# Expert weights of a mixture-of-experts stage in 8 KB runs: two rows for each of two experts per transfer, in place of one row for each of four

## The reference

```python
def _ec_moe(h, w_router, w_gate, w_up, w_down):
    B, L, _ = h.shape
    cap = EC_FACTOR * L // N_EXPERTS
    aff = jax.nn.softmax((h @ w_router).astype(jnp.float32), axis=-1)
    vals, idx = lax.top_k(jnp.swapaxes(aff, 1, 2), cap)
    bidx = jnp.arange(B)[:, None, None]
    xs = h[bidx, idx]
    hid = jax.nn.silu(jnp.einsum('becd,edf->becf', xs, w_gate)) * jnp.einsum('becd,edf->becf', xs, w_up)
    y = jnp.einsum('becf,efd->becd', hid, w_down) * vals[..., None].astype(h.dtype)
    return jnp.zeros_like(h).at[bidx, idx].add(y.astype(h.dtype))
```

## Time and profile before

| what | value |
|---|---|
| median of 3 runs | 1529.62 us (1526.79 to 1532.09) |
| profiled execution, its own time | 1532.12 us |
| profiled execution, its span | 1530.1 us |
| mean granted TensorE clock | 0.933 of full |
| TensorE matmul busy | 1292.4 us, 84% of the span |
| VectorE, ScalarE, GpSimd busy | 637.5, 498.0, 106.8 us |
| moved by DMA | 376.69 MB, of which 201 MB are expert weights |

### The profile page before, as it was taken

How to read it: one execution, slowest core, us unless ns; L and a number is a source line. 1 busy time by engine, 2 the same in 40 slices (tenths; PEclk the granted TensorE clock), 3 DMA queues, 4 the chain that set the end, 5 groups by cost and what they waited for, 6 DMA issues and landing times.

```text
span 1530.1 us, 22584 instructions
## 1 busy us (share of the span) xinstructions
PE 1292.4 (84%) x9336; PEld 960.6 (63%) x9336; DVE 637.5 (42%) x941; ACT 498.0 (33%) x756; POOL 106.8 (7%) x117
## 2 busy tenths in 40 slices
PE   5999999875555555655699999999999999999997
PEld 2388667521111111111477999999999987999996
DVE  2625665400100100100377656556545448566554
ACT  2424424400000000000437544445343438544443
POOL 0010010100000000000037000000000018000000
PEclk8999999898888887877899999999999999999999
DMA  9533619999999999999832465665566741355662
GB/s 366 201 97 83 237 71 356 418 409 418 419 419 419 418 419 421 416 420 420 306 111 70 152 193 165 186 199 164 179 191 183 216 141 57 109 168 168 198 198 68
DMA packets 137966, 376.69 MB, mean 246 GB/s; under 512 B 9423, under 2 KB 56960, under 8 KB 137703
## 3 DMA queue, kind: packets, MB, share of 16 engines
q1 hardware_dynamic: 137894, 375.68, 67.9%
HBM read 373.55 MB, written 1.05 MB: 245 GB/s over the span
## 4 chain that ended last, share of the span: by engine, by line
PE 64%; DMA 25%; DVE 4%; ACT 3%; SPq 2%; POOL 1%; issue 1%; ACTq 0%; DVEq 0%
PE psum L1937 16%; PE psum L1939 16%; PE psum L1938 16%; DMA ring<-in_w_down 6%; DMA work<-in_w_gate 4%; DMA work<-in_w_up 3%; PE psum L2278 3%; DMA ring<-in_w_up 3%; DMA tokens<-in_w_down 3%; DMA ring<-in_w_gate 3%; SPq L579 1%; PE psum L1873 1%; DMA early<-in_w_up 1%; POOL work L763 1%; PE psum L2107 1%; PE psum L2375 1%
## 5 line engine op out<-in xcount | busy, mean ns | idle before, releaser
L1937 PE MATMUL psum<-parts 128*128 128x256 f32 (+1 forms) x1672 | 497.2, 297 | 11.7 <-DVE parts L1585 9.5
L1938 PE MATMUL psum<-parts 128*128 128x256 f32 (+1 forms) x1672 | 494.8, 296 | 0.0
L1939 PE MATMUL psum<-parts 128*128 128x256 f32 (+1 forms) x1672 | 494.7, 296 | 0.0
L1579 DVE TENSOR_TENSOR parts<-ring,parts 128x1024 fp32r<-128x1024 f32 x232 | 280.8, 1227 | 170.7 <-ACT parts L1047 170.0
L1937 PEld LDWEIGHTS psum<-parts 128*128 128x128 f32 x1672 | 322.2, 193 | 22.5 <-issue 13.9
L1938 PEld LDWEIGHTS psum<-parts 128*128 128x128 f32 x1672 | 322.4, 193 | 7.1
L1939 PEld LDWEIGHTS psum<-parts 128*128 128x128 f32 x1672 | 322.1, 193 | 7.3
L1047 ACT CAST parts<-ring 128x1024 fp32r<-128x1024 f32 x232 | 239.6, 1045 | 249.1 <-PE psum L1939 209.3
L2278 PE MATMUL psum<-ring,work 128*32 128x512 f32 x576 | 95.8, 801 | 75.8 <-DMA ring<-in_w_gate 31.1
L1037 ACT ACTIVATE work<-psum 128x1024 f32<-128x1024 f32 x4 | 4.1, 1023 | 382.0 <-PE psum L2278 382.0
L1562 DVE TENSOR_TENSOR work<-work,psum 128x1024 f32<-128x1024 f32 x4 | 4.9, 1221 | 266.1 <-ACT work L1037 266.1
(11 more groups left out here) (357 smaller groups left out, 1396.8 us busy)
## 6 DMA issues: line engine op xcount, KB each, us to landing
ring<-in_w_qkv_b SPq DMA_DIRECT2D x72, 512.0 KB, 4.3
ring<-in_w_gate SPq DMA_DIRECT2D x16, 2048.0 KB, 22.2
work<-in_w_up SPq DMA_DIRECT2D x12, 2048.0 KB, 23.3
ring<-in_w_down SPq DMA_DIRECT2D x12, 2048.0 KB, 23.3
ring<-in_w_ada SPq DMA_DIRECT2D x44, 512.0 KB, 8.1
ring<-in_w_gate SPq DMA_DIRECT2D x44, 512.0 KB, 3.9
ring<-in_w_up SPq DMA_DIRECT2D x44, 512.0 KB, 5.3
ring<-in_w_down SPq DMA_DIRECT2D x44, 512.0 KB, 4.3
```

What stands on the lines that cost most here:

```text
L1579: dve.tensor_tensor(part_of(lo_slots, t, n), ring[:, slot_2(t), 0:n], part_of(hi_slots, t, n), ALU.subtract).then_inc(lo_ready, 1)
L1937: pe.matmul(out, lhsT[0], rhs[0], start=start, stop=False, skip_group_check=True)
L1938: pe.matmul(out, lhsT[0], rhs[1], start=False, stop=False, skip_group_check=True)
L1939: return pe.matmul(out, lhsT[1], rhs[0], start=False, stop=stop, skip_group_check=True)
```

## The change

The eight rows `8p` to `8p+7` of a weight matrix now belong to partition `p`, so that rows `8p + 2i` and `8p + 2i + 1`, which lie behind each other in HBM, are one run of 8 KB. A quad is still 2 MB, but holds two such rows for each of two experts: quads come in pairs (experts 0 and 1, experts 2 and 3), and a pair holds what contraction steps `2i` and `2i+1` need for all four experts. `by_expert` therefore takes two quads at once, runs the matmuls of two steps and adds eight to `tiles_done` at their end.

The rest follows the row order: contraction step `k` is now the rows `8c + k`. Transposes of `xn` and `hd`, the two `mod` calls for the feed-forward scale and shift, and the view `xn_by_k` read every eighth column (32 bytes apart) where they read neighbouring ones. The router's weights load as one run per partition. The host-side columns for gain and bias are laid out accordingly.

```diff
-        xn_by_k = [xn[:, t].rearrange("p (k c) -> p k c", k=KD) for t in range(TT)]
+        xn_by_k = [xn[:, t].rearrange("p (c k) -> p k c", k=KD) for t in range(TT)]
...
-                    sp.dma_start(w_rout, d["w_router"][0].rearrange("(k p) e -> p k e", p=P)).then_inc(route_loaded, 16)
+                    sp.dma_start(w_rout, d["w_router"][0].rearrange("(p k) e -> p k e", p=P)).then_inc(route_loaded, 16)
...
             def load_quad(expert, q):
-                name, k = (("w_gate", "w_up")[q % 2], q // 2) if q < 2 * KD else ("w_down", q - 2 * KD)
+                both, half = q // 2, q % 2
+                name, pair = (("w_gate", "w_up")[both % 2], both // 2) if both < KD else ("w_down", both - KD)
                 out, full, _ = homes[home_of[q]]
-                sp.dma_start(out, d[name][0, bass.ds(expert, EG), P * k:P * k + P, :].rearrange("j p n -> p j n")).then_inc(full, 16)
+                rows = d[name][0, bass.ds(expert + 2 * half, 2), :, :].rearrange("j (p r) n -> p j (r n)", r=KD)
+                sp.dma_start(out.rearrange("p j n -> p (j n)").rearrange("p (j m) -> p j m", j=2),
+                             rows[:, :, 2 * D * pair:2 * D * pair + 2 * D]).then_inc(full, 16)
...
-            def turn(src, ready, bank=0):
+            def turn(src, ready, bank=0, by_eights=False):
...
-                        ins = pe.transpose(ps[bank + k // 2][:, at:at + P], src[:, t, P * k:P * k + P], ident[:, :])
+                        rows = src[:, t].rearrange("p (c k) -> p k c", k=KD)[:, k, :] if by_eights else src[:, t, P * k:P * k + P]
+                        ins = pe.transpose(ps[bank + k // 2][:, at:at + P], rows, ident[:, :])
...
-                    ins = pe.matmul(ps[MOD_BANK[i]][:, 2 * k:2 * k + 2], modrow[:, P * k:P * k + P], pick_row, start=True, stop=True)
+                    row = modrow[:, P * k:P * k + P] if i < 2 else modrow.rearrange("p (c k) -> p k c", k=KD)[:, k, :]
+                    ins = pe.matmul(ps[MOD_BANK[i]][:, 2 * k:2 * k + 2], row, pick_row, start=True, stop=True)
...
-                def by_expert(bank, lhsT, w, k):
-                    for n in range(2):
-                        for j in range(EG):
-                            rows = slice(CAP * j, CAP * j + CAP)
-                            ins = pe.matmul(ps[bank + n][rows, :], lhsT[:, k, rows], w[:, j, 512 * n:512 * n + 512],
-                                            start=(k == 0), stop=(k == KD - 1))
-                    ins.then_inc(tiles_done, EG)
+                def by_expert(bank, lhsT, pair):
+                    ws = [quad(), quad()]
+                    for k in (2 * pair, 2 * pair + 1):
+                        for n in range(2):
+                            for j in range(EG):
+                                rows = slice(CAP * j, CAP * j + CAP)
+                                w = ws[j // 2][:, 2 * (j % 2) + k % 2, 512 * n:512 * n + 512]
+                                ins = pe.matmul(ps[bank + n][rows, :], lhsT[:, k, rows], w, start=(k == 0), stop=(k == KD - 1))
+                    ins.then_inc(tiles_done, 2 * EG)
...
-                for k in range(KD):
-                    by_expert(0, xs, quad(), k)
-                    by_expert(2, xs, quad(), k)
+                for pair in range(KD // 2):
+                    by_expert(0, xs, pair)
+                    by_expert(2, xs, pair)
...
-                    ins = pe.transpose(ps[6 + k // 4][:, P * (k % 4):P * (k % 4) + P], hd[:, P * k:P * k + P], ident[:, :])
+                    ins = pe.transpose(ps[6 + k // 4][:, P * (k % 4):P * (k % 4) + P], hd.rearrange("p (c k) -> p k c", k=KD)[:, k, :], ident[:, :])
...
-                for k in range(KD):
-                    by_expert(4, hdT, quad(), k)
+                for pair in range(KD // 2):
+                    by_expert(4, hdT, pair)
```

More of the change, by code:

```diff
@@ L2213, in _ @@
             pe.wait_ge(x_mixed, TT)
-            turn(xn, xt_ready, X_BANK)
+            turn(xn, xt_ready, X_BANK, by_eights=True)
             pe.wait_ge(route_loaded, 48)
@@ L2586, in laid_out @@
     column(C_GMIX, a["norm_mix_g"][0])
-    column(C_GFFN, a["norm_ffn_g"][0])
+    cols[:, C_GFFN:C_GFFN + KD] = a["norm_ffn_g"][0].reshape(P, KD)
     column(C_MIX2, a["norm_mix_2"].reshape(-1))
@@ L2593, in laid_out @@
     column(C_ADA, a["b_ada"][0])
+    for m in (3, 4):
+        cols[:, C_ADA + KD * m:C_ADA + KD * m + KD] = a["b_ada"][0][D * m:D * m + D].reshape(P, KD)
     column(C_FIN1, a["norm_final_g"])
```

## The result

The changed kernel takes 1537.67 us (median of 6 runs, 1537.37 to 1539.93) where the kernel before takes 1529.76 (6 runs): ratio 1.0061, with an interval of 1.0048 to 1.0074. It is slower, and outside the forecast range.

The account below looks back on a forecast made before the run. The prediction took the expert stage to run at the pace of the DMA engines, with slack in TensorE. Its terms, -10.3 + 3.2 + 0.5 + 0.5 = -6.1 us, gave a median of 1523.5 us, range 1520 to 1527.5.

Parts of the forecast that it names:

- Every eighth column: TensorE's strided reads in two `mod` calls and the turning of `xn`, ahead of the expert stage: +0.5 us.
- if 304.00 moves by over 1 us, the strides: Sign: if the expert stage's first matmul, at 304.00 us before, moves over 1 us, the strided reads were misjudged.
- The upper bound: Most that TensorE's strided reads in `mod` and `turn` were said to cost: 5.8 us, if they double.
- strided reads cost: Rival: TensorE's strided loads double, stage begins 5.3 us later than summed; -0.8 us in all, 1528.8; chance 0.15.
- cover: Stage start: the eleventh DMA is in time by 1.4 to 4 us before the engines run dry.
- The copies: ScalarE's cast and GpSimd's subtraction before the gather: even doubled, 2 + 4.8 us are covered by 8.1 us.
- The rate: Expert-stage transfers with 8 KB runs: 429 GB/s, 0.107 us less per quad, 10.3 us less over 96 quads.
- the rate does not move: Rival: engines are held by something that counts bytes, so the rate stays; +4.2 us, 1533.8; chance 0.14.
- slower transfers: Rival: partitions reading 32 KB apart in HBM slow the stage; whole change +17.1 us, 1546.7; chance 0.07.
- The last pair: Stage end: 32 matmul records where 16 stood, on the path to the second block: +3.2 us, bounds 1.9 to 5.2.
- The first pair: Stage start: the eleventh DMA waits for quads 0 and 1, leaving a hole of 0 to 1.3 us; 0.5 taken.
- Pairs between: Mid-stage: homes freed up to 8.5 us later, covered by transfers already in flight; priced at 0.

Follow-up runs that it names:

- the first experiment: Kernel before, with only the two `mod` calls for feed-forward scale and shift reading every eighth column: 1539.40 us, ratio 1.0067.
- the kernel with the row in order: Changed kernel, with ScalarE's copy out of PSUM writing `modrow` in the new column order so `mod` reads contiguous columns: 1528.91 us, ratio 0.9998.
- the one with the fill: Changed kernel with `modrow` written in order, plus three unused matmuls between the waits for each group's last pair: 1525.19 us, ratio 0.9973.
- pairs alone: Kernel before, 4 KB runs kept, but TensorE waits for and frees two quads at a time: 1532.97 us, ratio 1.0031.
- 8-byte steps: Kernel before, with the two `mod` calls for scale and shift reading every second column, single quads: 1529.93 us, one execution.
- the long runs alone: Kernel before, with only the transfers changed to 8 KB runs, single quads, no strided reads: 1522.88 us, ratio 0.9954.

## Why the prediction was wrong

**The step that failed is "Every eighth column".** The prediction took 0.5 us for the strided reads of `mod` and `turn`, "near the low end", because a load with its matmul took 122 ns and so "something else than the read sets the pace". The calls doubled: 3.9 us more, and with what came behind them the stage starts 10.3 us later, counted from the first call. The prediction had named the sign, "if 304.00 moves by over 1 us, the strides": it moved to 313.29. The argument was of the wrong kind. It showed that the pace was slower than one column per cycle, not that there was room in it for a read at half speed.

**The upper bound was too low as well.** 5.8 us counted the calls of `mod` and `turn` themselves. It held nothing for the clock, and half of the damage is there: 2.9 us in the two pieces behind the first call, and about 1.3 behind the second. So `mod` alone is worth 8.1 us up to the turning of `xn`, and 10 us (8 to 12.5) of the whole by the first experiment (0.67%). The prediction had the rival "strided reads cost", with its sign on this term right and its place too (a hole in the DMA), but priced it at -0.8 us in all.

**There was hardly any cover.** In the span the stage's first matmul comes 9.3 us later and the pair adds 1.7, so the eleventh DMA goes out 11.0 us later; the supply resumes 10.4 us later, and only 0.6 is hidden. The prediction counted 1.4 to 4 us of cover at this place. A window of the kernel before shows the DMA engines below their 420 GB/s there already, with single quads and no stride:

```profile
308.00:309.00 1.00, 1.00 (x16) 0.29 (x11) 0.00 (x0) 0.00 (x0) 0.00 (x0) 1.00 0.88 340
```

Nor do the transfers ahead of the stage give cover, since they wait for TensorE as well: the loads of w_out go out at 243.71, 13.4 us behind the start of the first `mod` call, where it was 239.83 and 8.5.

**Turning `xn`: right. The copies: 0.7 us where nothing was taken.** The turn takes 2.08 us against 1.98. ScalarE's cast of `xn` went from 1.98 to 4.00 us, GpSimd's subtraction from 4.76 to 5.79, as these rows of the timeline of the kernel after show:

```profile
287.35 4.00 ACT L1023 CAST parts<-tokens 128x1024 fp32r<-128x1024 f32 x2
...
291.44 5.79 POOL L745 TENSOR_TENSOR parts<-tokens,parts 128x1024 fp32r<-128x1024 f32 x2 [34.35 <-ACT parts L1023]
...
296.39 0.87 DVE L1541 CAST work<-work 16x32 f32<-16x32 uint32 x1
```

The sum of both, 3.1 us, is inside the 8.1 us that the prediction gave them up to the gather. But the last row lies between, on the chain to the gather: VectorE's copy of the top-k indices. In the kernel before it starts when GpSimd has long ended (286.12):

```profile
288.06 0.17 DVE L1538 CAST work<-work 16x32 f32<-16x32 uint32 x1
```

In the kernel after GpSimd ends at 297.23 and the copy at 297.26; it takes 0.7 us more. In the kernel with the row in order it takes 1.31 us and in the one with the fill 0.90, and there too it ends within 0.03 us of GpSimd's subtraction. In all seven kernels that split `xn` without a stride it takes 0.17. That the copy is held until GpSimd is done is read from these ends alone. By them, 0.7 of the 2.2 us between the turning of `xn` and the stage are the slower cast's. Another 0.9 are the router's matmuls behind the turn, 4.60 us against 3.72, while PEclk falls to 0.65 at 284 to 286 us; this fall is not the stride's alone, since kernels that turn `xn` without one have 3.95 (pairs alone) and 4.34 us (8-byte steps) there.

**The rate: right in kind, a little large.** 429 GB/s were forecast, and 427 to 428 measured; the gain is 8.6 us and not 10.3, mostly because it was taken over all 96 quads. The first ten land before TensorE needs them, so only 86 count. Packets fell by 25,473; 24,576 were forecast. The rivals "the rate does not move" and "slower transfers" fell with the long runs alone. By the Trainium skill's page "DMA: Bandwidth & Descriptors", section "Why small descriptors are slow", the estimate was 1.2%; this case's trace has 420 to 427 GB/s, 1.7%.

**The last pair: right place, 1.4 us short.** +3.2 was taken ("the first half slow and the second fast") and +4.6 measured, within its bounds of 1.9 to 5.2. In the kernel after PEclk stays low for most of the 32 records.

**The first pair: 0.5 us taken, about 1.2 found.** From the stage's first matmul to the start of the last pair there are 429.67 us in the kernel after, against 437.09 before: 7.4 less, where 86 quads gain 8.6. What is left, 1.2 us, is about the upper bound of 1.3; with the row in order it is 1.3. This is from single executions, which scatter: the same distance is 439.2 us with the pairs alone and 439.1 in the kernel with 8-byte steps, which has none.

**Pairs between: right.** 427 GB/s with 4.9 us per quad to the end leave no hole. SP now orders further ahead, as this part of the page's issues (KB each, median us to landing) shows, against 22.2 us in the earlier trace rows. By the steady 4.9 us per quad it gains nothing:

```profile
ring<-in_w_gate SPq DMA_DIRECT2D x12, 2048.0 KB, 26.0
...
ring<-in_w_down SPq DMA_DIRECT2D x12, 2048.0 KB, 32.7
```

With the measured terms, -8.6 + 4.6 + 10.4, the change is slower; with the strided loads away, only the faster transfers and the two ends are left, and they nearly cancel (ratio 0.9998). With one end mended the gain shows.

## What to carry to other kernels

A layout that makes a transfer faster puts its stride somewhere else. List each reader of it that is on the path and find a row for a read at that stride, or try it by itself; the same permutation cost 0.67% in TensorE's loads and nothing in ScalarE's copy out of PSUM. If a change lengthens a stretch in which TensorE idles or does only tiny matmuls, price its end and the pieces behind it at the lower clock too. And when a rate improves, count only the transfers that someone waits for, then look at what each end of the stage does with a supply that runs dry sooner.

## What the runs showed that was not expected

- TensorE's load of 128 float32 columns is nearly free of charge at a stride of 8 bytes (2.05 us for 16 with their matmuls against 1.95) and doubled at 16 and 32 bytes (3.89 and 3.96), where six and five or six of its records fall in a microsecond, at the full and at the half clock. The transposes of `xn`, which read at 32 bytes too, hardly change (1.98 to 2.08 us for 16). Why they are spared was not tried.
- ScalarE's cast from SBUF doubled at 32 bytes (1.98 to 4.00 us for two), while its copy from PSUM at the same stride kept its 1.01 us. A VectorE copy of 16 x 32 values, which reads no strided data, grew from 0.17 to 0.87 and 1.31 us where it ran beside GpSimd's subtraction, and ended with it.
- The granted clock stays 1.00 behind a call of 1.95 us of two-column matmuls and is 0.50 at the end of one of 3.9 us with stride and of one of 4.85 us without: a fully busy row for TensorE is no warrant for its clock.
- Three matmuls whose result nobody reads, put in a wait, brought 2.5 us on the path: 3.64 us instead of 6.11 for the 32 records behind it.
